# A hybrid decoder layer on one core: half of the pieces of two down-projections as seven block products

## The reference, cut to what matters

```
h = rmsnorm(x, g_pre_ffn[l])
up = causal_dwconv(h @ w_up[l], w_fconv[l], b_fconv[l])
gate, val = jnp.split(up, 2, axis=-1)
x = x + rmsnorm((jax.nn.gelu(gate, approximate=True) * val) @ w_down[l], g_post_ffn[l])
```

## Time and profile before

| | us |
|---|---|
| median of 3 runs | 1735.39 |
| lowest, highest | 1735.25, 1735.74 |
| span of the profiled execution | 1732.8 |
| both down-projections that the change touches, in that span | 87.04 each |

### The profile page before, as it was taken

One profiled execution on the slowest core, in us unless ns is written; L12 is line 12 of the kernel. 1 busy time (PEld: TensorE's weight loads), 2 busy tenths in 40 slices (PEclk: granted clock), 3 DMA queues, 4 the chain that ended last, 5 costly groups with the idle time before them and its releaser, 6 DMA issues.

```text
span 1732.8 us, 25350 instructions
## 1 busy us (share of the span) xinstructions
PE 1724.4 (100%) x8968; PEld 1470.6 (85%) x8968; DVE 1142.9 (66%) x1437; ACT 919.5 (53%) x1175; POOL 157.3 (9%) x183
## 2 busy tenths in 40 slices
PE   9999999999999999999999999999999999999998
PEld 8888888888888888888888888888888888888886
DVE  7766665466788874446566677775467776467766
ACT  7656655443666763344456665553355555245553
POOL 0012210000334520000000000000000000000000
PEclk9999999999999999999999999999999999999999
DMA  9645556566566565556554465556456556545552
GB/s 340 200 141 156 156 196 234 190 237 195 157 193 188 170 242 192 192 187 243 195 177 172 137 194 185 180 179 231 155 185 194 184 181 237 174 151 188 194 213 103
DMA packets 214267, 330.09 MB, mean 190 GB/s; under 512 B 5696, under 2 KB 161984, under 8 KB 206784
## 3 DMA queue, kind: packets, MB, share of 16 engines
q1 hardware_dynamic: 208576, 318.53, 54.5%
q10 hardware_dynamic: 5632, 10.75, 1.7%
HBM read 327.16 MB, written 2.10 MB: 190 GB/s over the span
## 4 chain that ended last, share of the span: by engine, by line
PE 99%; DVE 0%; issue 0%; ACT 0%; DVEq 0%; POOL 0%; POOLq 0%
PE ps L506 51%; PE ps L569 40%; PE ps L522 3%; PE ps L781 1%; PE ps L709 1%; PE ps L631 1%; PE ps L620 0%; PE ps L601 0%; PE ps L738 0%; PE ps L714 0%; PE ps L731 0%; PE ps L625 0%; PE ps L739 0%; PE ps L869 0%; PE ps L853 0%; PE ps L595 0%
## 5 line engine op out<-in xcount | busy, mean ns | idle before, releaser
L1540 DVE TENSOR_TENSOR wsp<-raw,wsp 128x2048 fp32r<-128x2048 f32 (+2 forms) x303 | 671.7, 2235 | 326.3 <-ACT wsp L1054 323.1
L1054 ACT ACTIVATE wsp<-raw 128x2048 fp32r<-128x2048 f32 (+2 forms) x304 | 558.0, 1855 | 284.4 <-PE ps L569 278.1
L506 PE MATMUL ps<-asp,wsp 128*128 128x512 f32 x3064 | 542.4, 339 | 0.0
L506 PEld LDWEIGHTS ps<-asp,wsp 128*128 128x128 f32 x3064 | 469.8, 188 | 70.2 <-DVE asp L2001 0.3
L569 PE MATMUL ps<-wsp,hsp 128*128 128x512 f32 x2292 | 522.9, 389 | 0.0
L569 PEld LDWEIGHTS ps<-wsp,hsp 128*128 128x128 f32 x2292 | 430.0, 188 | 89.0
L506 PE MATMUL ps<-hsp,wsp 128*128 128x512 f32 (+1 forms) x1936 | 349.7, 340 | 0.0
L506 PEld LDWEIGHTS ps<-hsp,wsp 128*128 128x128 f32 x1936 | 297.5, 188 | 42.9
L569 PE MATMUL ps<-wsp,asp 128*128 128x512 f32 x768 | 175.6, 389 | 0.0
L1065 ACT ACTIVATE cr<-ps 128x256 f32<-128x256 f32 x185 | 69.2, 380 | 197.2 <-PE ps L506 180.8
L569 PEld LDWEIGHTS ps<-wsp,asp 128*128 128x128 f32 x768 | 144.0, 188 | 29.8
(11 more groups left out here) (264 smaller groups left out, 935.6 us busy)
## 6 DMA issues: line engine op xcount, KB each, us to landing
raw<-in_w_up SPq DMA_DIRECT2D x88, 1024.0 KB, 5.6
raw<-in_w_in SPq DMA_DIRECT2D x64, 1024.0 KB, 5.4
raw<-in_w_down SPq DMA_DIRECT2D x44, 1024.0 KB, 5.4
raw<-in_w_in SPq DMA_DIRECT2D x32, 768.0 KB, 4.4
raw<-in_w_o_mla SPq DMA_DIRECT2D x16, 1024.0 KB, 5.0
raw<-in_w_o_lru SPq DMA_DIRECT2D x16, 1024.0 KB, 5.1
raw<-in_w_out SPq DMA_DIRECT2D x16, 1024.0 KB, 5.0
raw<-in_w_ukv SPq DMA_DIRECT2D x8, 1024.0 KB, 5.4
```

The source lines that it names most:

```text
L506: mm = pe.matmul(ps[:, bank, 0:w], lhs(part, k), x[:, 0:w], start=(f and part == 0), stop=(l and n == 1))
L1054: act.activation(wsp[:, p0 % SLOTS, 0, 0:n], raw[:, p0 % SLOTS, 0:n], ACT.Copy).then_inc(hi_done, 1)
L1540: dve.tensor_tensor(wsp[:, slot, 1, 0:n], raw[:, slot, 0:n], wsp[:, slot, 0, 0:n].bitcast(F32), ALU.subtract).then_inc(lo_done, 1)
```

## The change

In groups 0 and 1, the down-projection is cut in another way. The output is made in two halves h of 1024 columns. Within a half, hidden tiles are taken in pairs k0, k1, eight pairs, so a 1 MB piece is two hidden tiles by 1024 columns. Four pairs ("plain", 0, 2, 4, 6) are multiplied as before, 24 matmuls each. For the other four (1, 3, 5, 7) the product of the 2 x 2 blocks of hidden values (token block by hidden tile) and the 2 x 2 blocks of weights (hidden tile by 512 columns) is made by a scheme of seven products in place of eight. It needs sums of blocks on both sides:

- Four sums of hidden blocks per pair (`forms`). GpSimd makes them in `form_sums` from `HID`, ScalarE and VectorE split them (`form_high`, `form_low`). They lie where x3 was; x3 is written to DRAM (`x3_kept`) in the first rounds of group 0 and read back during group 2.
- Four sums of weight blocks per pair. A "first" piece is the fetched pair; TensorE uses three of its blocks (9 matmuls). A "made" piece in the next slot holds the four sums (12 matmuls). SyncE fetches one block of 512 columns twice into the made slot (512 KB), GpSimd issues a DMA that adds two neighbouring blocks of the first slot to it (`two_blocks`, 512 KB from SBUF to SBUF with an adding write), and VectorE makes the other two sums, one after the other (`sums_rest`).

So a half has 12 pieces in the order plain, plain, first, made, first, made, plain, first, made, first, made, plain, and a down-projection has 24, called piece 0 to piece 23 below. The products that are shared among outputs have four banks of their own, the plain results the other four, and the two sets change places between the halves. `products_out` combines the product banks on VectorE, with one bank first copied by ScalarE (`q1_keep`), after the last made piece of a half; `plain_out` adds the plain banks. The last group is as it was, apart from its counts.

The diff, cut to its core (counters and semaphores that only follow from it are left out):

```diff
+DN_HALF = [("plain", 0), ("plain", 2), ("first", 1), ("made", 1), ("first", 3), ("made", 3),
+           ("plain", 4), ("first", 5), ("made", 5), ("first", 7), ("made", 7), ("plain", 6)]
...
+    if _count % 16 == 0:
+        PH_DN.append(Phase(PH_UP[-1], 1, [0] * 24))
+    else:
+        PH_DN.append(Phase(PH_UP[-1], _count // 4, [0] * 4))
...
-                rounds(sp, dn, dn_rows)
+                if fn == 16:
+                    for c in range(24):
+                        kind, pair = DN_HALF[c % 12]
+                        k, c0 = f0 + 2 * pair, (c // 12) * 1024
+                        if kind == "made":
+                            slot = (dn.p0 + c) % SLOTS
+                            sp.wait_ge(lo_done, dn.p(0, c) - SLOTS + 1)
+                            sp.dma_start(raw[:, slot, 0:1024].rearrange("p (a t) -> p a t", a=2),
+                                         w_dn[:, k:k + 1, c0:c0 + 512].to_broadcast([P, 2, 512])).then_inc(landed[slot], 16)
+                        else:
+                            piece(dn, 0, c, 2, 1024, w_dn[:, k:k + 2, c0:c0 + 1024])
+                else:
+                    rounds(sp, dn, dn_rows)
...
-                    pe.wait_ge(y_out, 8 * n - 4)
+                    pe.wait_ge(dn_out, 16 * n - 4)
...
+                def form_mm(bank, lhs, slot, block, first, last):
+                    for t, (part, low) in enumerate(TERMS):
+                        mm = pe.matmul(ps[:, bank, :], lhs(low), wsp[:, slot, part, quarter(block)],
+                                       start=(first and t == 0), stop=(last and t == 2))
+                    return mm
...
+                    for at in range(12):
+                        kind, pair = DN_HALF[at]
+                        c, k0, k1 = 12 * h + at, 2 * pair, 2 * pair + 1
+                        slot = c % SLOTS
+                        arrive(dn, 0, c)
+                        if kind == "plain":
+                            pe.wait_ge(hid_lo, f0 + k1 + 1)
+                        if at == 0 and h == 1:
+                            pe.wait_ge(dn_out, 16 * n + 4)
+                        if kind == "first":
+                            pe.wait_ge(hid_lo, f0 + k1 + 1)
+                            pe.wait_ge(fm_lo, 4 * n + pair // 2 + 1)
+                        if at == 2 and 2 * n + h:
+                            pe.wait_ge(dn_out, 16 * n + 8 * h)
...
+                        elif kind == "first":
+                            form_mm(q1, block(k0, 0), slot, 1, at == 2, at == 9)
+                            form_mm(dn_plain_bank(h, 0, 1), block(k1, 0), slot, 3, False, False)
+                            mm = form_mm(dn_plain_bank(h, 0, 0), form(pair, 3), slot, 2, False, False)
+                        else:
+                            form_mm(q5, form(pair, 1), slot, 0, at == 3, at == 10)
+                            form_mm(q7, form(pair, 0), slot, 1, at == 3, at == 10)
+                            form_mm(q6, form(pair, 2), slot, 2, at == 3, at == 10)
+                            mm = form_mm(dn_plain_bank(h, 1, 1), block(k1, 1), slot, 3, False, False)
+                        mm.then_inc(gemm_step, 1)
...
+                        act.dma_start(x3_kept, a_tok).then_inc(x3_spilled, 16)
+                    up_round(1)
+                    if n == 0:
+                        act.wait_ge(x3_spilled, 16)
...
+                    act.dma_start(a_tok, x3_kept).then_inc(x3_back, 16)
...
+                def made_high(c):
+                    slot = (dn.p0 + c) % SLOTS
+                    act.wait_ge(gemm_step, dn.g(0, dn.used[c - SLOTS]) if c >= SLOTS else dn.g0)
+                    act.wait_ge(sums_made, dn_sums(n, c) + 1)
+                    act.activation(wsp[:, slot, 0, :], raw[:, slot, :], ACT.Copy).then_inc(hi_done, 1)
...
+                def q1_keep(h):
+                    act.wait_ge(gemm_step, dn.g(0, dn.used[12 * h + 10]))
+                    if h:
+                        act.wait_ge(dn_out, 16 * n + 8)
+                    kept = y_tok[:, 0, 1024 * h + 512:1024 * h + 1024] if n == 0 else Q1_KEPT
+                    act.activation(kept, ps[:, 4 * (1 - h), :], ACT.Copy).then_inc(q1_out, 1)
...
+                def sums_rest(c):
+                    dve.wait_ge(lo_done, dn.p(0, c) + 2 - SLOTS)
+                    dve.wait_ge(two_sums[dn_sums(n, c + 1) % 2], 16 * (dn_sums(n, c + 1) // 2) + 16)
+                    own.link(dve.tensor_tensor(raw_blocks(c + 1, 2), raw_blocks(c + 1, 0), raw_blocks(c, 2), ALU.add))
+                    dve.tensor_tensor(raw_blocks(c + 1, 3), raw_blocks(c + 1, 2), raw_blocks(c, 3), ALU.add).then_inc(sums_made, 1)
...
+                def products_out(h):
+                    _, q6, q7, q5 = (ps[:, 4 * (1 - h) + b, :] for b in range(4))
+                    done = 16 * n + 8 * h
+                    dve.wait_ge(gemm_step, dn.g(0, dn.used[12 * h + 10]))
+                    dve.wait_ge(q1_out, 2 * n + h + 1)
+                    if n == 0:
+                        v, w, q1 = V_SUM, y_at(h, 1, 1), y_at(h, 0, 1)
+                    else:
+                        v, w, q1 = V_SUM, W_SUM, Q1_KEPT
+                    dve.tensor_tensor(v, q1, q6, ALU.add).then_inc(dn_out, 1)
+                    if n:
+                        own.mark(dve.tensor_tensor(y_at(h, 0, 1), y_at(h, 0, 1), q1, ALU.add))
+                    dve.wait_ge(dn_out, done + 1)
+                    dve.tensor_tensor(w, v, q7, ALU.add).then_inc(dn_out, 1)
+                    if n == 0:
+                        dve.tensor_tensor(y_at(h, 0, 0), q5, v, ALU.subtract).then_inc(dn_out, 1)
+                        dve.wait_ge(dn_out, done + 2)
+                        dve.tensor_tensor(y_at(h, 1, 0), q5, w, ALU.subtract).then_inc(dn_out, 1)
+                    else:
+                        for m in range(2):
+                            dve.tensor_tensor(y_at(h, m, 0), y_at(h, m, 0), q5, ALU.add).then_inc(dn_out, 1)
+                        dve.wait_ge(dn_out, done + 2)
+                        own.mark(dve.tensor_tensor(y_at(h, 1, 1), y_at(h, 1, 1), w, ALU.add))
+                        for m, sub in enumerate((v, w)):
+                            dve.wait_ge(dn_out, done + 3 + m)
+                            own.mark(dve.tensor_tensor(y_at(h, m, 0), y_at(h, m, 0), sub, ALU.subtract))
+                def plain_out(h):
+                    dve.wait_ge(dn_out, 16 * n + 8 * h + 4)
+                    if n:
+                        own.wait()
+                    for at, (m, b) in enumerate([(0, 0), (0, 1), (1, 0), (1, 1)]):
+                        if at == 3:
+                            dve.wait_ge(gemm_step, dn.g(0, dn.used[12 * h + 11]))
+                        else:
+                            dve.wait_ge(dn_done, 6 * n + 3 * h + at + 1)
+                        y = y_at(h, m, b)
+                        dve.tensor_tensor(y, y, ps[:, dn_plain_bank(h, m, b), :], ALU.add).then_inc(dn_out, 1)
...
+                        kinds = ["plain" if at >= 24 else DN_HALF[at % 12][0] for at in range(c, c + 2)]
+                        if c == LEAD:
+                            sums_rest(c)
+                        if c == 15:
+                            plain_out(0)
+                        if kinds[0] == "first":
+                            first_low(c)
+                        else:
+                            lo(dn, 0, c)
+                        if kinds[1] == "first":
+                            sums_rest(c + 1)
+                        if c in (13, 25):
+                            products_out(c // 24)
+                        if c == 25:
+                            plain_out(1)
...
+            def form_sums(n, pair):
+                pool.wait_ge(hid_out, pair * 4 + 16 * n + 4)
+                if not isinstance(pair, int) or 4 * n + pair:
+                    pool.wait_ge(fm_lo, pair + 4 * n)
+                f7_f5, f6, f3 = (FORM[:, a * P:b * P] for a, b in ((0, 2), (2, 3), (3, 4)))
+                both = scr[:, 12 * T:14 * T].rearrange("p (e t) -> p e t", e=2)
+                own.link(pool.tensor_tensor(f7_f5.rearrange("p (e t) -> p e t", e=2), both[:, 0, :].rearrange("p (e t) -> p e t", e=2),
+                                            both[:, :, P:2 * P], ALU.subtract))
+                own.link(pool.tensor_tensor(f6, FORM[:, P:2 * P], A11, ALU.subtract))
+                pool.tensor_tensor(f3, f6, A12, ALU.add).then_inc(fm_raw, 1)
...
+            def two_blocks(dn, n, c):
+                slots = [(dn.p0 + at) % SLOTS for at in (c, c + 1)]
+                for at in (c, c + 1):
+                    pool.wait_ge(landed[(dn.p0 + at) % SLOTS], dn.landed(0, at))
+                pool.dma_start(raw[:, slots[1], 0:1024], raw[:, slots[0], 512:1536], accum_op=ALU.add).then_inc(two_sums[dn_sums(n, c + 1) % 2], 16)
...
+                def up_pair(r):
+                    own.n, own.off = n0 + 8 * n, r * 2
+                    up_round(r * 2)
+                    up_round(r * 2 + 1)
+                    form_sums(n, r)
```

(9 more changed lines are left out.)

## The result

| | before | after |
|---|---|---|
| median, us | 1735.3 (4 runs, 1734.9 to 1735.7) | 1798.2 (4 runs, 1797.0 to 1799.7) |
| span of the profiled execution, us | 1732.8 | 1796.2 |

A forecast was written before the change was run, and what follows sets the result against it. TensorE, with 99% of the chain, was taken as the bound. Waits of 15.6 and 16.8 us plus clock 2, less 10.9 saved, gave + 23.5 us: 1735.4 to 1759, range 1738 to 1782.

The forecast's parts named there:

- The saving: Both down-projections: 48 fewer matmuls at 0.2267 us each, 10.9 us of TensorE, all on the chain.
- Costed at nothing: Hidden sums of the other pairs, and x3's write and return beside up-projection fetches: all covered, no time added.
- Wait A: Before piece 2 of each group: first adding transfer issued behind the last pair's hidden sums, TensorE waits 4.0 us.
- Waits B: Pieces 3 to 10: small waits of 0.35 to 0.5 us for VectorE, 0.85 at piece 7, 3.6 in all.
- Wait C: Change of halves, before piece 12: products_out late behind low parts and piece 15's sums, 7.1 us, 7.7 in group 1.
- Piece 21 is ready 3 us early: Second half of a down-projection: after piece 12 the rest runs without a wait, piece 21 having 3 us to spare.
- Wait D: Before the next up-projection: the second half's products_out ends late behind low parts, 0.9 us, 1.5 in group 1.
- The clock: TensorE drops to 1.2 GHz after some 4 to 5 us of waiting; lower speed costs 1 us per group.
- the transfer's 4.4 us: Adding DMA of 512 KB from SBUF to SBUF: lands in 4.4 us, taken from the 768 KB row.
- the second fetch, taken at 3.8: Doubled 512 KB fetch into the made slot: 3.8 us, including 0.4 for often following a 1 MB fetch closely.
- The rival with the slow transfer: Adding transfer takes 7 us, an adding one perhaps passing the engines slower: + 44 us, 1780; chance 0.12.
- The rival with the clock: TensorE at half speed for all of piece 12 and after early waits too: + 8 to 11 more, 1769; chance 0.05.

The follow-up runs named there:

- the floor: Changed kernel with the four weight sums, the second fetch and the adding transfer left out (output differs): 1726.34 us, ratio 0.9949.
- a hold: Kernel before, TensorE held once per down-projection after its eighth piece by GpSimd memsets: long version 1753.88 us, short version (2.2 us) 1741.22 us.
- the run with the clock kept: Changed kernel with 40 extra matmuls into a free bank while TensorE waits between pieces 11 and 12: 1794.42 us, ratio 1.0344.
- the copying transfer: Changed kernel with the GpSimd DMA copying 512 KB in place of adding, two sums left out (output differs): 1785.23 us, ratio 1.0288.
- the first GpSimd run: Changed kernel with one GpSimd instruction of 1024 columns per pair in place of second fetch and adding transfer, orders unchanged: 1760.68 us, ratio 1.0150.

## Why the prediction was right about the sign and wrong about the size

- **The saving**, 10.9 us: right. The pieces run at 0.2267 us per matmul wherever the clock is full, and the floor shows 8.6 of it.
- **Costed at nothing**: nearly right. The up-projections are within 0.3 us of before; all that is not the weight sums costs 2.3 us.
- **Wait A**, forecast 4.0: 4.84 (4.68 in group 1). No fetch ran beside the transfer, and it landed in 4.7 us, forecast 4.4; it went out 1.0 us later than forecast. This step is right.
- **Waits B**, forecast 3.6: 5.2 (4.8), of another kind. The small waits for VectorE's width (0.35 to 0.5 each) did not come: behind a long wait TensorE is at the lower clock and VectorE keeps up. The whole is piece 7, forecast 0.85. Its second fetch went out at 1192.0, 1.3 us later than forecast. From there to the issue of the transfer it took 5.5 us, 1.7 more than the 3.8 I had taken, and the transfer 4.6 more than 4.4, with a fetch of 1 MB and one of 512 KB beside it. That makes 7.6 us, of which 3.0 are covered, as TensorE was itself later.
- **Wait C**, forecast 7.1 and 7.7: 11.2 and 12.0. Place, releaser and order were as told. The second fetch for piece 15 took 6.4 us to the issue of the transfer, for 4.3, and the transfer 7.0 for 4.4, 4.7 more in all.
- **A wait not forecast**, before piece 21: 6.76 (2.70). "Piece 21 is ready 3 us early" failed through a second fetch that landed after 6.6 us and a transfer of 9.4.
- **Wait D**, forecast 0.9 and 1.5: 0.73 and 0.85. The numbers are near, but by then TensorE was late by the wait before piece 21, which the forecast did not have, so they owe something to luck.
- **The clock**, forecast 1 per group: about 9 per group. Two things were wrong: that only waits longer than 4 to 5 us count, and that a fall costs 1 to 2 us once. Every one of the four longer waits brought it, that of 2.7 us in group 1 too, and each cost 1.5 to 3.0 us (2.0 and 2.2 behind a hold, 2.7 at C by the run with the clock kept).

So the step that failed is the sizing of terms whose mechanism was right. The first is the path to a late sum: the transfer's 4.4 us was held constant, and it is right with no fetch beside it and short by 2.6 to 5 us beside fetches, and the second fetch, taken at 3.8, took 5.5 and more to the issue of the transfer. With these the waits of group 0 are 28.8 us where 15.6 were forecast, and those of group 1 are 25.1 where 16.8 were. The second is the clock, about 18 us in place of 2. In group 0 the waits miss by 13.2 and the longer busy time by 9.0 (8.2 of clock, 0.8 of matmul ends), together 22.2: the 33.4 measured less the 11.2 (15.6 + 1 - 5.4) forecast. In group 1 they miss by 8.3 and 9.0, of 29.6 measured and 12.4 forecast.

The rival with the slow transfer, at 7 us and a chance of 0.12, has 53.2 us of waits, where 53.8 were measured. The sum is close by luck: in it A and D are each 2.6 us longer than forecast, which they were not, and it lacks the wait before piece 21. With the small clock term it stops at 1780. The rival with the clock, at a chance of 0.05, adds 8 to 11 us where about 16 were missing. Both came together, and I had priced them apart.

The fit that the Trainium skill gives on its page "DMA: Bandwidth & Descriptors", section "Anatomy of one DMA — SWDGE (gpsimd) path" (an estimate of 3.2 us for 512 KB), suits the copying transfer with nothing beside it, 2.8 at the shortest and 3.5 at the median of all. The adding one was 4.5 at best.

That a transfer stretches beside fetches is read from which fetches were under way, for the adding and the copying one; no run moved all of them away and kept the rest. The run without the second fetch shows that most of it stays beside the fetches of 1 MB alone: in it the transfers for pieces 8, 15 and 22 landed after 7.8, 6.2 and 9.1 us, where the changed kernel has 9.0, 7.0 and 9.4 (4.5 to 4.8 without fetches in both).

## What to carry to other kernels

Saved matmuls pay only if what prepares them keeps TensorE fed: set each preparing engine's us per piece against TensorE's, at the tightest pair of neighbours too, and apply the trick only to as many pieces as fit (here two pairs in a half gave all of their saving, and four gave less than none in every order that was tried). Don't put a chain of fetch, transfer and sum between a freed slot and its use, nor an eviction behind it, when, as here, a direct sum on the engine costs 1.2 us. Price a wait of TensorE at its length plus 1.5 to 3 us of clock once it is a few us long, in each place that it occurs, and price the landing of a transfer by what else moves at that time.

## What the hardware showed that was not expected

- A DMA from SBUF to SBUF that adds 512 KB landed in 4.5 to 4.7 us with no fetch under way when it went out and in 7.0 to 9.4 beside fetches, and these stretched too: one issued at 1194.7 landed after 7.5 us, and the 512 KB one behind it after 9.5. The copying one landed in 2.8 to 7.7, median 3.5.
- GpSimd's one addition of 1024 columns (2.65 us on average in the first GpSimd run) held up VectorE instructions with two SBUF inputs that met it; an addition of 0.69 us became 2.8.
- TensorE's clock was at 0.50 behind waits of 4.8 us. It also fell in waits of 2.7 and 2.35 us and in one of 2.2, but not in the twin of that one, nor in one of 3.33 us; 1.9 to 2.2 us were lost behind a single hold, whether it was 2.2 (the first one) or 6.8 us long.
